# Key units open linear attention, and h and the weights' high part get other addresses

## The reference

```python
h = x @ w_in
q, k, v, r, a = jnp.split(h, [GLA_QK, 2 * GLA_QK, 2 * GLA_QK + GLA_VD, 2 * GLA_QK + 2 * GLA_VD], axis=-1)
log_a = jax.nn.log_sigmoid((a @ w_a2 + b_a).astype(jnp.float32)) / GLA_TAU
...
cum = jnp.cumsum(log_a, axis=2)
tot = cum[:, :, -1]
k_dec = k * jnp.exp(tot[:, :, None] - cum).astype(k.dtype)
```

## Time and profile before

| | us |
|---|---|
| median of 3 runs (1758.9 to 1759.49) | 1759.13 |
| profiled execution | 1757.15 |
| its span, first to last instruction | 1755.3 |
| TensorE busy | 1741.2 |
| VectorE busy | 1142.4 |
| ScalarE busy | 953.7 |
| granted TensorE clock, mean | 0.999 |

### The profile page before, as it was taken

The page is one execution under the profiler, slowest core; times in us unless marked ns, Lnnn a source line. Parts: engine busy times, 40 slices in busy tenths (PEclk is TensorE's granted clock), DMA queues, the critical chain, the costliest instruction groups (busy, mean ns, idle before and its releaser), DMA issues.

```text
span 1755.3 us, 32869 instructions
## 1 busy us (share of the span) xinstructions
PE 1741.2 (99%) x14102; PEld 1708.1 (97%) x14102; DVE 1142.4 (65%) x1842; ACT 953.7 (54%) x1521; POOL 123.0 (7%) x130
## 2 busy tenths in 40 slices
PE   9999999999999999999999999999999999999998
PEld 9989999997999999999999999999999999999998
DVE  7776998575689875855547765554656556775544
ACT  7665777465467664744434454444454444764443
POOL 1002000110020002000011020001000002020003
PEclk9999999999999999999999999999999999999999
DMA  6434555544445555455554545555455554245552
GB/s 236 140 103 163 174 193 184 189 169 157 142 153 205 185 188 183 168 178 177 173 179 152 173 156 175 175 180 169 156 174 168 192 184 165 97 174 187 186 187 97
DMA packets 85057, 297.75 MB, mean 170 GB/s; under 512 B 10512, under 2 KB 13456, under 8 KB 84912
## 3 DMA queue, kind: packets, MB, share of 16 engines
q1 hardware_dynamic: 84176, 294.85, 50.0%
q10 hardware_dynamic: 736, 0.80, 0.2%
HBM read 294.57 MB, written 1.05 MB: 168 GB/s over the span
## 4 chain that ended last, share of the span: by engine, by line
PE 90%; DVE 5%; ACT 2%; POOL 1%; DMA 1%; issue 0%; SPq 0%; DVEq 0%; POOLq 0%
PE ps L1493 27%; PE ps L1492 27%; PE ps L1494 27%; PE ps L1528 1%; PE ps L1523 1%; DVE w_lo L932 1%; PE ps L1524 1%; POOL acc L905 1%; PE ps L1549 1%; PE ps L1799 1%; DVE y L987 1%; ACT w_hi L444 1%; DMA raw<-stream 1%; PE ps L1503 0%; DVE y L968 0%
## 5 line engine op out<-in xcount | busy, mean ns | idle before, releaser
L932 DVE TENSOR_TENSOR w_lo<-raw,w_hi 128x1024 fp32r<-128x1024 f32 x557 | 690.7, 1248 | 326.0 <-ACT w_hi L444 207.9
L444 ACT ACTIVATE w_hi<-raw 128x1024 fp32r<-128x1024 f32 x557 | 580.0, 1050 | 171.9 <-DMA raw<-stream 150.1
L1492 PE MATMUL ps<-a_hi,w_hi 128*128 128x256 f32 (+1 forms) x2088 | 591.4, 283 | 0.5 <-DVE w_lo L932 0.4
L1493 PE MATMUL ps<-a_lo,w_hi 128*128 128x256 f32 (+1 forms) x2088 | 590.0, 283 | 0.0
L1494 PE MATMUL ps<-a_hi,w_lo 128*128 128x256 f32 (+1 forms) x2088 | 586.9, 281 | 0.0
L1492 PEld LDWEIGHTS ps<-a_hi,w_hi 128*128 128x128 f32 x2088 | 392.9, 188 | 1.7 <-DVE w_lo L932 1.2
L1494 PEld LDWEIGHTS ps<-a_hi,w_lo 128*128 128x128 f32 x2088 | 393.3, 188 | 0.0
L1493 PEld LDWEIGHTS ps<-a_lo,w_hi 128*128 128x128 f32 x2088 | 392.2, 188 | 0.5
L1492 PE MATMUL ps<-h_hi,w_hi 128*128 128x256 f32 (+1 forms) x1336 | 379.1, 284 | 0.3 <-DVE y L948 0.3
L1494 PE MATMUL ps<-h_hi,w_lo 128*128 128x256 f32 (+1 forms) x1336 | 377.7, 283 | 0.0
L1493 PE MATMUL ps<-h_lo,w_hi 128*128 128x256 f32 (+1 forms) x1336 | 377.7, 283 | 0.0
(11 more groups left out here) (269 smaller groups left out, 1805.6 us busy)
## 6 DMA issues: line engine op xcount, KB each, us to landing
raw<-stream SPq DMA_DIRECT2D x557, 512.0 KB, 3.3
x<-xT SPq DMA_DIRECT2D x2, 512.0 KB, 4.8
out<-x SPq DMA_DIRECT2D x8, 128.0 KB, 1.8
work<-pT ACTq DMA_DIRECT2D x2, 256.0 KB, 3.1
par<-params SPq DMA_DIRECT2D x1, 283.5 KB, 11.3
tmp<-causal ACTq DMA_DIRECT2D x1, 208.0 KB, 2.5
con<-consts SPq DMA_DIRECT2D x1, 194.5 KB, 9.4
tmp<-pos SPq DMA_DIRECT2D x1, 128.0 KB, 9.4
```

The lines of the kernel that those rows point to most:

```text
L444: nc.scalar.activation(w_hi[:, u % SLOTS, :], raw[:, u % SLOTS, :], ACT.Copy).then_inc(w_hi_ready, 1)
L932: nc.vector.tensor_tensor(w_lo[:, u % SLOTS, :], raw[:, u % SLOTS, :], w_hi[:, u % SLOTS, :].bitcast(F32), ALU.subtract).then_inc(w_lo_rea ...
L1492: nc.tensor.matmul(dst, wh, xh, start=first, stop=False, skip_group_check=True)
L1493: nc.tensor.matmul(dst, wh, xl, start=False, stop=False, skip_group_check=True)
```

## The change

Three edits. In linear attention the phases `gla_a` and `gla_k` change places. The keys open and wait, tile by tile, for b's low parts; `gla_a` follows as a plain unit into bank 5, then one value unit, then the two logit matmuls, then three value units ahead of the suffix sums, where there were four. ScalarE and VectorE follow that order. `h_gap` grows and `h_lo_gap` shrinks, so that `h_hi` begins at 128 modulo 256 and `h_lo` at 64, as `a_hi` and `a_lo` do. A gap of 128 bytes ahead of `w_hi` puts it at 0 modulo 256; `w_lo` stays at 128, and a gap behind it keeps x, y, a and b where they were modulo 256.

```diff
-           ("gla_a", 1), ("gla_k", 4), ("gla_v", 8), ("gla_q", 4), ("gla_r", 8), ("gla_o", 8),
+           ("gla_k", 4), ("gla_a", 1), ("gla_v", 8), ("gla_q", 4), ("gla_r", 8), ("gla_o", 8),
...
-for _unit, _next in ((109, 43), (218, 152), (407, 475)):
+for _unit, _next in ((109, 43), (218, 152), (407, 475), (119, 124)):
...
+GLA_A_BANK = 5
...
         raw = sb("raw", [P, SLOTS, UNIT])
+        sb("w_gap", [P, 32])
         w_hi = sb("w_hi", [P, SLOTS, UNIT], F32R)
+        sb("x_gap", [P, 32])
...
-        sb("h_gap", [P, 16])
+        sb("h_gap", [P, 48])
         h_hi = sb("h_hi", [P, NF, T], F32R)
-        sb("h_lo_gap", [P, 32])
+        sb("h_lo_gap", [P, 16])
         h_lo = sb("h_lo", [P, NF, T], F32R)
...
             act.dma_start(g_wa2[0:32, :], wa2).then_inc(in_wa2, 16)
-            u = BASE["gla_a"]
-            act.wait_ge(unit_done, u + 1)
-            nc.scalar.activation(g_aT[0:32, :], ps[0:32, u % BANKS, 0:SEQ], ACT.Identity,
-                                 bias=ccol("one16")[0:32, :]).then_inc(aT_ready, 1)
-            hi_next(u)
             for i in range(4):
-                u = BASE["gla_k"] + i
-                hi_next(u)
-            act.wait_ge(unit_done, BASE["gla_v"])
+                hi_next(BASE["gla_k"] + i)
+            act.wait_ge(unit_done, BASE["gla_a"])
             for m in range(2):
                 nc.scalar.activation(g_k[:, m, :], ps[:, m, :], ACT.Copy).then_inc(gk_copied, 1)
+            u = BASE["gla_a"]
+            hi_next(u)
+            act.wait_ge(unit_done, u + 1)
+            nc.scalar.activation(g_aT[0:32, :], ps[0:32, GLA_A_BANK, 0:SEQ], ACT.Identity,
+                                 bias=ccol("one16")[0:32, :]).then_inc(aT_ready, 1)
...
             for i in range(5):
-                lo_next(BASE["gla_a"] + i)
+                lo_next(BASE["gla_k"] + i)
+            lo_next(BASE["gla_v"])
             dve.wait_ge(ln_ready, 1)
...
-            for i in range(4):
+            for i in range(1, 4):
                 lo_next(BASE["gla_v"] + i)
...
             pe.wait_ge(pp_copied, 4)
-            opening("gla_a", TOK, b_hi, b_lo, x_hi_ready, x_split, X_SPLIT["ple0"], 1)
+            pe.wait_ge(sig_ready, 7)
...
                     k = 2 * (i % 4) + kk
+                    if phase == "gla_k":
+                        pe.wait_ge(x_split, X_SPLIT["ple0"] + k + 1)
...
-            pe.wait_ge(aT_ready, 1)
             for i in range(4):
                 by_token("gla_k", i, 0)
-
+            u = BASE["gla_a"]
+            pe.wait_ge(w_lo_ready, u + 1)
+            for k in range(KD):
+                ins = three(ps[:, GLA_A_BANK, 0:SEQ], *tile(u, k), b_hi[:, k, TOK], b_lo[:, k, TOK], k == 0, k == KD - 1)
+            ins.then_inc(unit_done, 1)
+            by_token("gla_v", 0, 2)
+
+            pe.wait_ge(aT_ready, 1)
             pe.wait_ge(in_wa2, 16)
...
-            for i in range(4):
+            for i in range(1, 4):
                 by_token("gla_v", i, 2)
```

More of the change, by code:

```diff
@@ L1944, in _ @@
             pe.wait_ge(pp_copied, 4)
-            opening("gla_a", TOK, b_hi, b_lo, x_hi_ready, x_split, X_SPLIT["ple0"], 1)
+            pe.wait_ge(sig_ready, 7)
             def by_token(phase, i, first_bank):
                 u = BASE[phase] + i
-                slot = u % BANKS
                 pe.wait_ge(w_lo_ready, u + 1)
```

## The result

The changed kernel takes 1763.76 us in the median, where the kernel before took 1758.27 on the same chips: a ratio of 1.003, with a 95% interval of 1.0021 to 1.0040. One of its eight timed runs took 2107.47 us at a granted clock of 0.752; the ratio leaves it out, and the median without it is 1763.70. The kernel is slower by more than the 3.5 us that the prediction took as the least that can be told from no change, and above its range. In the profiled executions it is 1763.51 against 1757.15 us, with spans of 1761.7 and 1755.3: +6.4 us. The third rival had named this way and nearly this time (1763.2). The granted clock is at the upper level in both (0.999 and 1.000), and the table of engines counts the same instructions on each.

A forecast was written before the change was run, and what follows sets the result against it. TensorE, busy 1741.2 of 1755.3 us, was taken as the bound, so only its waits or matmul spacing could change the time. Terms -2.5 - 3.2 + 1.1 = -4.6 took the 1759.13 us median to 1754.5, range 1748.5 to 1760.5.

The forecast's parts named there:

- The third rival: Weight parts 128 bytes apart lock badly: units of `a` take 2.84 us, +6.6 us, time 1763.2 us; chance 0.13.
- Edit 1: Reordering in linear attention: keys opening instead of `gla_a` removes 2.48 us of TensorE waiting, forecast -2.5 us.
- Both covers: Linear attention: a value unit hides `gla_a`'s eviction; three units still cover `la` before the suffix, by 1.2 us.
- Edit 2: Moving `h` to a's places speeds output products (1.0 us) and down products (1.8 and 0.4 us), forecast -3.2 us.
- I take the rate of `a`: Down products: with h's parts 64 bytes apart, a pair takes 5.60 us instead of 5.64, and 6.00 instead of 6.02.
- Edit 3: Moving `w_hi` 128 bytes on puts one more 256-column up stage at its slow unit time, forecast +1.1 us.
- the mapping: With `w_hi` moved, `a` was to get b's address pattern two tiles on, and b a's; 2.80 or 2.83 us a unit.
- I cost it by r: Cost of moving `w_hi`, read from the streamed operand's place relative to the weights loading beside it, in 64-byte steps.
- the prediction's last sentence: The prediction is wrong if matmul distance depends on the weights' place otherwise than by the load running beside them.
- the bound of +3.3: Worst case for moving `w_hi`: all four 256-column up stages at the slow unit time, +3.3 us.
- With 272 columns I take no change: Moving `w_hi` was to leave the unit times of stages with 272 columns as they were.
- The 0.6 us that the range allowed: Added at the range's upper end, 1760.5 us, for address places that no profile row shows.

The follow-up runs named there:

- experiment 5: Against experiment 1: both weight parts, w_hi and w_lo, moved 64 bytes on, to 192 modulo 256; 1757.15 us in one run.
- experiment 2: Against the kernel before: only w_hi moved, to 0 modulo 256, with old order and old places of h; 1765.53 us, ratio 1.0050.
- experiment 1: Against the kernel before: only the reordering in linear attention, all addresses as before; 1754.29 us, ratio 0.9987.
- Experiment 6: Against experiment 1: w_hi moved 64 bytes on, to 192 modulo 256, w_lo kept at 128; 1759.31 us, ratio 1.0006.
- experiment 7: Against experiment 1: w_hi moved 192 bytes on, to 64 modulo 256, w_lo kept at 128; 1761.44 us in one run.
- experiment 3: Against the kernel before: only h moved to a's places (h_hi 128, h_lo 64), old order; 1758.18 us, ratio 1.0009.
- experiment 8: Against experiment 1: h moved to b's places (h_hi 128, h_lo 192 modulo 256); 1756.42 us, ratio 0.9992.
- experiment 10: Against experiment 1: seven keep_busy matmuls instead of six ahead of the last up product; 1754.23 us, ratio 0.9978.
- experiment 4: The changed kernel without the shift of w_hi, which is back at 128 modulo 256; 1755.30 us, ratio 0.9993 against the kernel before.
- experiment 9: Against experiment 1: h_hi at 128 and h_lo at 0 modulo 256, 128 bytes apart; 1752.74 us in one run.
- experiment 12: The kernel of experiment 9, unchanged, timed against the kernel before; 1753.90 us, ratio 0.9979.

## Why the prediction was wrong, step by step

**The reading of the bound was right.** Nothing but the distance of the matmuls and a few waits moved the time: with 14102 matmuls in both kernels, spacing alone took 9 us. The cause was right too, as far as it said that the streamed operand's place relative to the weights counts (experiment 5). What the prediction drew from the rule of the Trainium skill ("TensorE: Matmul & The Clock Gate", "Part 2: What happens when you issue a matmul"), that no place matters relative to the weights, is not so here: experiment 2 moves one weight part, and the time rises by 9.1 us. Whether it is the read of weights beside the running matmul that costs, which that section of the Trainium skill rules out, or something else that depends on the addresses, no run shows.

**Edit 1 was right.** -2.5 us forecast; -2.6 in the trace of experiment 1, -2.2 between the medians. Both covers held, the second with 1.1 us of the 1.2. In the changed kernel the stretch is 0.15 us shorter than in experiment 1; that part comes with the shifted weights, beside which the key and value units take 2.76 to 2.79 us in place of 2.78 to 2.81.

**Edit 2 failed at "I take the rate of `a`" for the down order.** The output products were right for mla_ob (2.80) and half right for the other two with 256 columns (2.83). The down pairs were to fall to 5.60 and rose to 5.68. In the down order a tile stays for 12 matmuls, in `a`'s for three, so that the same pair of addresses gives two different sequences, and the one doesn't carry over to the other. The six down products together lost 1.1 - 0.3 = 0.8 us in place of gaining 2.2, inside the bounds given (1.8 us of loss at the most). In place of -3.2, edit 2 alone gave between +0.8 (trace) and +1.7 (medians). In the changed kernel, beside the shifted weights, the down products lost 1.3 and mla_ob stayed at 2.84.

**Edit 3 failed at the mapping.** "I cost it by r" let only the load beside the running matmul count, so that `a` would get `b`'s pattern, at +1.1 us. This is the step that put the forecast out of its range. `a` got 2.84, a time that neither had shown. Experiments 6 and 7 then tried the same rule at two more places and it fell there too, as the prediction's last sentence allowed. Measured alone the edit costs 9.1 us (8.4 between traces), far above the bound of +3.3, since this bound knew only the two unit times seen before. "With 272 columns I take no change" was wrong as well: +2.5 us. The 0.6 us that the range allowed for places that no row shows had nothing behind it, nor had the 0.7 at its lower end for the 272-column down products, which a pair's 6.02 against 6.00 puts at 0.4; experiment 3 gave 0.3.

**The third rival had the cause and the rate for `a`, and its time is partly chance.** Units of `a` at 2.84 were to cost 6.6 us; they cost 5.4. The 272-column stages of `a` and `b` (+2.5) and the down products (+1.3) came on top and weren't in its sum: it gave +4.1 in all, where the profiled executions differ by 6.4 and the medians by 5.5. That 1763.2 and 1763.8 lie so near is also due to the kernel before, whose median is 1758.3 over all its runs and was 1759.1 in the first three. Its chance, 0.13, was too small: against it stood only the mapping, which no row had shown.

**What stays open.** Which matmul and which load have to stand how for a short distance. The table above has four places of `w_hi`, and the experiments four of `h`; no rule that was tried explains them. What decides between 2.800 and 2.827 at the entry of a stage wasn't found either. That the cost arises between the streamed read and the weight load is argued, not shown: the runs show only that their relative place and the distance between the weight parts change it.

## What to carry to other kernels

Where TensorE is busy for 99%, read the distance of matmul starts by stage: it shows costs that waits and busy shares don't. Take a pattern of addresses as something to be measured, and give a combination that no row shows a bound beyond the best and worst times seen, for it can be worse than either. A rate read in one order of matmuls need not hold for another order on the same addresses.

## What the runs showed that was not expected

A gap of 128 bytes between two weight buffers, with the same instructions, is worth 0.5% (1756.44 against 1765.53 us). 24 matmuls of 256 columns, tile after tile, took 2.800, 2.813, 2.827, 2.840 or 2.867 us, and of 272 columns 2.987, 3.000, 3.013, 3.027 or 3.040: the times lie about 0.013 us apart.

With both weight parts at the same place modulo 256, a stage that reads `a` has one of two unit times, 2.800 or 2.827, keeps it to its end, and in another kernel with the same places takes the other one (up0, up1 and up5 in experiments 5, 8 and 10). Others do so too: in experiment 3 mla_ob is at 2.800 and the other two output products with 256 columns at 2.827, and in experiment 7 `a` at 272 columns has 2.987 in one stage and 3.013 in the next. An up stage of 41 such units differs by 41 x 0.027 = 1.1 us. With the weight parts 128 bytes apart `a` had one time only, 2.840. The spread of the runs goes with it: the kernel before ran at 1755.70 to 1759.38 us in the group of experiments 1 to 4, that of experiment 2 at 1765.49 to 1765.62, and the changed kernel at 1763.51 to 1763.99. That the two unit times cause this spread wasn't shown, and two things speak for a second cause. Experiment 6 has all four up stages with 256 columns at 2.827 and still ran at 1758.82 to 1760.27 us. And the one kernel with two traces (experiments 9 and 12) took 1752.74 and 1753.66 us with the same unit times; 0.8 us of the difference arose before up0.
